# The last output product of a two-block transformer kernel as seven half-size products, with two of its weight sums on GpSimd

## The reference

```python
    merged = (jax.nn.sigmoid(g_diff) * (o_diff @ w_proj_diff[layer])
              + jax.nn.sigmoid(g_mla) * (o_mla @ w_proj_mla[layer]))
    x = x + merged @ w_out[layer]
return rms_norm(x, norm_final)
```

## Time and profile before

| what | value |
|---|---|
| time, median of 3 runs | 1087.87 us (1087.51 to 1088.33) |
| span of the profiled execution | 1085.8 us |
| PE busy | 1072.4 us (99% of the span) |
| DVE busy | 712.5 us (66%) |
| ACT busy | 420.2 us (39%) |
| POOL busy | 0.2 us |
| granted TensorE clock, mean | 0.999 |

### The profile page before, as it was taken

The page is one execution under the profiler, slowest core; times in us unless marked ns, Lnnn a source line. Parts: engine busy times, 40 slices in busy tenths (PEclk is TensorE's granted clock), DMA queues, the critical chain, the costliest instruction groups (busy, mean ns, idle before and its releaser), DMA issues.

```text
span 1085.8 us, 13595 instructions
## 1 busy us (share of the span) xinstructions
PE 1072.4 (99%) x5395; PEld 860.1 (79%) x5397; DVE 712.5 (66%) x1149; ACT 420.2 (39%) x661; POOL 0.2 (0%) x4
## 2 busy tenths in 40 slices
PE   9999999999999999999999999999999999999998
PEld 6777877977878888888888887887776777888886
DVE  6998877868678887854588745654568446464441
ACT  6513655334443223222222234744367443323232
POOL 0000000000000000000000000000000000000000
PEclk9999999999999999999999999999999999999999
DMA  8422122221213323234322234323121222033302
GB/s 279 126 78 79 47 71 79 71 86 39 79 60 106 117 79 105 59 89 129 122 78 88 65 94 143 98 97 117 44 78 40 78 78 78 1 116 117 102 35 78
DMA packets 100239, 95.59 MB, mean 88 GB/s; under 512 B 5952, under 2 KB 91216, under 8 KB 100176
## 3 DMA queue, kind: packets, MB, share of 16 engines
q1 hardware_dynamic: 100000, 94.71, 27.9%
q10 hardware_dynamic: 176, 0.02, 0.0%
HBM read 92.60 MB, written 2.10 MB: 87 GB/s over the span
## 4 chain that ended last, share of the span: by engine, by line
PE 91%; DVE 5%; ACT 2%; issue 1%; DMA 1%; SPq 0%; DVEq 0%; ACTq 0%
PE ring L1036 22%; PE ring L1038 22%; PE ring L1037 22%; PE bank L1036 3%; PE bank L1038 3%; PE bank L1037 3%; PE bank L1500 1%; PE bank L1295 1%; DVE w_lo L1929 1%; PE bank L1267 1%; DMA w_raw<-in_w_in 1%; PE bank L1200 1%; PE bank L1280 1%; PE bank L1524 1%; PE bank L1473 1%
## 5 line engine op out<-in xcount | busy, mean ns | idle before, releaser
L1036 PE MATMUL ring<-act_hi,w_hi 128*128 128x512 f32 (+2 forms) x808 | 320.2, 396 | 0.9 <-DVE xT L2312 0.5
L1038 PE MATMUL ring<-act_hi,w_lo 128*128 128x512 f32 (+2 forms) x808 | 313.5, 388 | 0.0
L1037 PE MATMUL ring<-act_lo,w_hi 128*128 128x512 f32 (+2 forms) x808 | 313.2, 388 | 0.0
L1588 ACT ACTIVATE w_hi<-w_raw 128x2048 fp32r<-128x2048 f32 (+5 forms) x96 | 159.8, 1665 | 249.7 <-PE ring L1038 200.6
L1929 DVE TENSOR_TENSOR w_lo<-w_raw,w_hi 128x2048 fp32r<-128x2048 f32 (+4 forms) x101 | 190.3, 1886 | 4.2 <-ACT w_hi L1588 3.9
L1036 PEld LDWEIGHTS ring<-act_hi,w_hi 128*128 128x128 f32 x808 | 151.8, 188 | 37.1 <-issue 3.9
L1038 PEld LDWEIGHTS ring<-act_hi,w_lo 128*128 128x128 f32 x808 | 151.7, 188 | 31.6
L1037 PEld LDWEIGHTS ring<-act_lo,w_hi 128*128 128x128 f32 x808 | 151.8, 188 | 31.3 <-issue 1.9
L1036 PE MATMUL ring<-hidH,w_hi 128*128 128x512 f32 x176 | 68.5, 389 | 0.0
L1037 PE MATMUL ring<-hidL,w_hi 128*128 128x512 f32 x176 | 68.5, 389 | 0.0
L1038 PE MATMUL ring<-hidH,w_lo 128*128 128x512 f32 x176 | 68.5, 389 | 0.0
(11 more groups left out here) (363 smaller groups left out, 1618.9 us busy)
## 6 DMA issues: line engine op xcount, KB each, us to landing
w_raw<-in_w_in SPq DMA_DIRECT2D x30, 1024.0 KB, 5.3
w_raw<-in_w_up SPq DMA_DIRECT2D x22, 1024.0 KB, 5.1
w_raw<-in_w_out SPq DMA_DIRECT2D x8, 1024.0 KB, 5.1
w_raw<-in_w_down SPq DMA_DIRECT2D x8, 768.0 KB, 4.7
w_raw<-in_w_down SPq DMA_DIRECT2D x8, 640.0 KB, 4.3
w_raw<-in_w_in SPq DMA_DIRECT2D x7, 512.0 KB, 4.7
xin<-in_xt SPq DMA_DIRECT2D x8, 256.0 KB, 4.1
xT<-in_xt SPq DMA_DIRECT2D x2, 1024.0 KB, 6.6
```

What stands on the lines that cost most here:

```text
L1036: pe.matmul(out, ah, bh, start=(first and n == 0), stop=False)
L1037: pe.matmul(out, ah, bl, start=False, stop=False)
L1038: mm = pe.matmul(out, al, bh, start=False, stop=(last and n == len(pairs) - 1))
L1588: return act.activation(out, src, func, **more)
```

## The change

The output product is made with seven products of half size (Strassen's scheme in Winograd's form) in place of eight. `merged` is cut into A11, A12 (channels 0-511 and 512-1023 of tokens 0-255), A21, A22 (of tokens 256-511), and `w_out` into B11, B12, B21, B22. Four sums of weights are formed on the chip: T1 = B12 - B11, T3 = B22 - B12, T2 = T3 + B11, T4 = B21 - T2 (128 x 2048 each), and four sums of activations: S3 = A11 - A21, S1 = A21 + A22, S2 = S1 - A11, S4 = A12 - S2 (128 x 1024 each). The products, in the order of the program, are

0: A11 B11; 1: S3 T3; 2: A12 B21; 3: S2 T2; 4: S1 T1; 5: S4 B22; 6: A22 T4 (with the signs folded into the sums).

Each is made for two groups of 128 tokens, with 12 matmuls a group: 168 in all, where there were 192. The four groups of the residual are still transposed (32 transposes): into the banks of products 2, 5 and 6 and into two ring tiles (`res`). Banks are shared by product n and n + 3, so DVE and ACT must read a bank before the product three later.

T3 and T2 are made on DVE (`t_sum`), **T1 and T4 on GpSimd**, all four S on DVE (`s_sum`). All forms and sums are split into hi and lo like the rest. The scheme's additions of products are on DVE (`s17`, `u_sum`, `v_sum`, `c_sum`, 128 x 512 each, one input from a bank). The scaling by the gain is now a step of its own from SBUF (`scaled`). B12, B22 and B21 are loaded by SP into a raw buffer and into the place of the activations' dead splits.

```diff
+        for c in range(4):
...
+            if c == 3:
+                stage("s_split", 3)
             for kind in ("pd", "pm"):
                 for i in (2 * c, 2 * c + 1):
+                    if (kind, i) == ("pm", 6):
+                        stage("t_sum", "T3")
                     in_tile(kind, i, f"pj{c}")
+                    if (kind, i) == ("pm", 6):
+                        split_form("T3")
+            if c == 1:
+                stage("s_sum", 3)
+
+        both("prod", 0)
         stage("m_flush")
...
+        split_form("B21")
+        stage("t_sum", "T2")
+        both("snap")
+        both("prod", 1)
+        stage("s_sum", 1)
+        stage("s_sum", 2)
+        split_form("T2")
+        stage("s_split", 2)
+        both("s17")
+        for t in range(2):
+            tile(("res", t))
+            stage("res", t)
+        both("prod", 2)
+        stage("c_sum", 2, 0)
+        stage("s_split", 1)
+        stage("c_sum", 2, 1)
+        split_form("T1")
+        stage("s_sum", 4)
+        each("sq_early", 0, 1)
+        both("prod", 3)
+        split_form("B22")
+        stage("s_split", 4)
+        both("u_sum")
+        both("prod", 4)
+        split_form("T4")
+        both("c_sum", 4)
+        both("v_sum")
+        each("sq_early", 2, 3)
+        both("prod", 5)
+        for t in range(2):
+            stage("scaled", t)
+            stage("c_sum", 5, t)
+        each("final", 0, 1)
+        each("scaled", 2, 3)
+        both("prod", 6)
+        for t in range(2):
+            stage("c_sum", 6, t)
+            stage("final", 2 + t)
...
+            wait_split(sp, B11 - 1)
+            quarter_in(raw[(B11 + 1) % 2], 0, 1, raw_in[(B11 + 1) % 2])
+            sp.wait_ge(tile_done, upto(("gm", KD - 1)))
+            quarter_in(b22, 1, 1, block_in[0])
+            quarter_in(b21, 1, 0, block_in[1])
...
+        @block.gpsimd
+        def _(pool):
+            pool.wait_ge(tile_done, upto(("gm", KD - 1)))
+            pool.wait_ge(raw_in[(B11 + 1) % 2], landed[B11 - 1] + 16)
+            pool.wait_ge(raw_in[B11 % 2], landed[B11])
+            pool.tensor_tensor(t1[:], raw[(B11 + 1) % 2][:], raw[B11 % 2][:], ALU.subtract).then_inc(pool_sum, 1)
+            pool.wait_ge(form_sum, 2)
+            pool.wait_ge(w_lo_done, B11 + 1)
+            pool.tensor_tensor(b21[:], b21[:], form_raw["T2"][:], ALU.subtract).then_inc(pool_sum, 1)
...
+                    if name == "T3":
+                        dve.wait_ge(block_in[0], 32)
+                        dve.wait_ge(pool_sum, 1)
+                        TT(form_raw["T3"][:], b22[:], form_raw["T3"][:], ALU.subtract).then_inc(form_sum, 1)
```

More of the change, by code:

```diff
@@ L176, in two_blocks @@
         gated_d, gated_m, merged, m_hi, m_lo = (sem(n) for n in ("gated_d", "gated_m", "merged", "m_hi", "m_lo"))
+        form_sum, pool_sum, s_sum, s_hi, s_lo = (sem(n) for n in ("form_sum", "pool_sum", "s_sum", "s_hi", "s_lo"))
+        prod_mm, snap, part_sum, c_sum = (sem(n) for n in ("prod_mm", "snap", "part_sum", "c_sum"))
         ssf_ready, xo_g, f_var, f_rs, out_act, out_dve, out_done = (
@@ L793, in two_blocks, with split_form, both @@
         attention("mla", 4, "ym", fill)
+        B11 = len(chunks)
+        chunk("B11", k_out2[:, 0:4, 0:512])
+        for name in ("T3", "B21", "T2", "T1", "B22", "T4"):
+            form(name)
+        PROD = ("B11", "T3", "B21", "T2", "T1", "B22", "T4")
+        def split_form(name):
+            stage("w_first", chunk_of[name])
+        def both(kind, *what):
+            for t in range(2):
+                stage(kind, *what, t)
         for c in range(4):
@@ L1542, in _ @@
                     channels(s, f"pj{i // 2}", P * (i % 2), (oH[:, at:at + 4, :], oL[:, at:at + 4, :]), nk=4, part=0 if kind == "pd" else 1)
[L1543 to L1556, removed]
-                        for j in range(4):
[L1558 to L1562, removed]
@@ new lines, in _ @@
+                elif kind == "prod":
+                    n, t = s[1:]
+                    at = slice(P * t, P * t + P)
+                    if n == 0:
+                        pe.wait_ge(m_lo, 4)
+                    elif n in (2, 6):
+                        pe.wait_ge(m_lo, KD)
+                    else:
+                        pe.wait_ge(s_lo, S_SPLITS.index(S_OF[n]) + 1)
+                    if n == 3:
+                        pe.wait_ge(snap, t + 1)
+                    elif n == 4:
+                        pe.wait_ge(part_sum, t + 1)
+                    elif n == 5:
+                        pe.wait_ge(c_sum, t + 1)
+                    elif n == 6:
+                        pe.wait_ge(part_sum, 2 * t + 4)
+                    to = bank[2 * (n % 3) + t]
+                    opened = n in RES_OF
+                    if opened:
+                        half, b0 = RES_OF[n]
+                        for j in range(4):
+                            pe.matmul(to[:, P * j:P * j + P], xT[:, 4 * half + j, b0 + P * t:b0 + P * t + P], ident,
+                                      start=(j == 0), stop=False, is_transpose=True)
+                    lh, ll = left_of(n)
+                    wh, wl = weights(PROD[n])
+                    product(to[:], [((lh[:, k, at], ll[:, k, at]), (wh[:, k, :], wl[:, k, :])) for k in range(4)],
+                            first=not opened).then_inc(prod_mm, 1)
+                elif kind == "res":
+                    b = 2 + s[1]
+                    out = open_bank(s)
+                    for j in range(4):
+                        mm = pe.transpose(out[:, P * j:P * j + P], xT[:, 4 + j, P * b:P * b + P], ident)
+                    mm.then_inc(tile_done, 1)
```

303 lines of the change are left out of this document (201 added, 102 removed).

## The result

The changed kernel takes 1092.26 us (median of 4 runs, 1091.68 to 1092.70), the kernel before in the same sessions 1088.1 us: a ratio of 1.004, 95% interval 1.0026 to 1.0054. It is 4.2 us slower; 3.6 was forecast.

A forecast was written before the change was run, and what follows sets the result against it. TensorE bounds the old stretch, DVE's queue the new end: 1081.35 + 0.8 + 4.2 = 1086.32 against 1082.69, 3.6 us slower. 1087.87 + 3.6 = 1091.5 us; range 1086.0 to 1093.2.

The forecast's parts named there:

- The bare gain of 4.7 us: Output product: 24 fewer matmuls save 5.44 us of TensorE, less 0.73 for the last addition on DVE.
- The queue that I had at 31.7 us: DVE's gapless work from 1040.06 to 1071.8, up to the fourth-last addition, making DVE end last.
- T1's 0.8 us: GpSimd's T1 holds the split of S3, delaying `pd` 6, T3 and the B21 split: 0.8 us.
- T4's 4.2 us: GpSimd's T4 gets in before S2, which starts at 1050.7 in place of 1046.5: 4.2 us in DVE's queue.
- The early gap: Contention with T4 taking DVE's gap before S2 at 1046.5: 3.6 us slower, chance 0.42.
- Rival 2: Contention, but T4 misses the gap before S2 and covers only S1's split: 2.0 us slower, chance 0.20.
- The price of a GpSimd sum: Length of a 128 x 2048 two-input sum on GpSimd: 4.2 us, the middle of 3.8 and 4.57.
- The exclusive end: GpSimd's sums and DVE instructions with two SBUF inputs can't run together; the second waits: 3.6 us slower in total.
- The clock: Rival 5: a 3 us TensorE stall might drop it to 1.2 GHz; nothing added, given 4 us of slack.
- the 4 of my sum: TensorE's slack against DVE by the time of a possible clock fall: 4 us.
- Transfers: B22 and B21 loads, issued together at 1022.4, stay hidden, B22 by 0.6 us before T3 wants it.

The follow-up runs named there:

- the kernel without the sums: Changed kernel with both GpSimd sums left out (products 4 and 6 use B22 and B21 instead): 1086.70 us, 0.9992 of the kernel before.
- T1 alone: Changed kernel with only the second GpSimd sum, T4, left out (product 6 uses B21): 1087.98 us, 1.0000 of the kernel before.
- S3's split late: Changed kernel with S3's split moved behind the reading of `pd` 7, so T1 runs beside bank reads only: 1091.97 us, 1.0039 of the kernel before.
- T4 alone: Changed kernel with only the first GpSimd sum, T1, left out (product 4 uses B22): 1091.27 us, 1.0030 of the kernel before.
- T4 after S2: Changed kernel with GpSimd's T4 also waiting for the sum S2: 1092.51 us, 1.0044 of the kernel before.
- the new order: Changed kernel with scalings ahead of the first final steps and both last additions ahead of the last two: 1090.44 us, 1.0021 of the kernel before.
- the three edits together: Changed kernel with T1 on DVE, GpSimd's T4 beside DVE's bank reads, and the end reordered: 1085.81 us, 0.9979 of the kernel before.

## Why the prediction was right

**TensorE's saving and the DVE queue.** The bare gain of 4.7 us shrinks to 1.34 because DVE ends last: shown by the kernel without the sums, 1.2 us ahead of before with nothing held. The queue that I had at 31.7 us takes 31.5 there, from 1040.65 to the end of the addition at 1071.47 (the third from the end; the prediction calls it the fourth).

**T1's 0.8 us.** Shown by T1 alone, 1.3 us. `pm` 6 waited 1.1 us, not 0.9. As a wait of TensorE it costs nothing (S3's split late); it stands for the delay of DVE's queue. **T4's 4.2 us.** Shown by T4 alone, 4.6 us, and in the row of S2, 4.3 us longer than S1. The early gap was the right one of the two contention cases, but for a wider reason than I gave: GpSimd doesn't need S2's wait to get in (T4 after S2). Rival 2 rested on the opposite.

**The price of a GpSimd sum** was the term mis-sized: 4.63 us in place of 4.2. The upper end, two DVE passes (4.57), was nearly right. The Trainium skill (GPSIMD Engine Reference, section 3.1) has 4497 ns for it; measured 4.63. With 4.63 both sums give 0.9 us more, 4.5 in all, against 4.2 measured in the medians and 4.7 between the two profiled ends (1087.40 and 1082.69). In the profiled execution 0.4 us is older than the change's stretch: the last gate tile is read at 1022.73 in place of 1022.34.

**The exclusive end.** Shown from both sides: a DVE instruction with two SBUF inputs is held, one with an input from a bank isn't, and a GpSimd copy holds too. The Trainium skill (SBUF — State Buffer, "Who interferes with whom") states this, of a DVE instruction with two SBUF inputs against a GpSimd instruction that reads SBUF, and the rows agree with it that the second one is held until the first is done: 1.09 us from GpSimd's end to the end of a 1.22 us instruction.

**The clock.** It did fall, for 12 matmuls: 5.3 us in place of 2.7, and TensorE had the slack that I argued with. An addition that does wait for TensorE starts 0.42 us behind the last matmul (1081.99 and 1082.41 in the new order, 1076.55 and 1076.97 in the three edits together). With T4 alone, at the full clock, DVE adds 4.10 us behind it (1079.38 and 1083.48): a slack of 3.7 us, near the 4 of my sum. In the changed kernel it adds 1.88 us behind it (1082.67 and 1084.55), so some 1.5 us were left. **Transfers** were hidden: T3 starts on DVE as soon as `pd` 7 is read, at 1030.0.

What was not settled: why the clock fell behind the stalls of 3.4 and 4.8 us and not behind that of 3.7, and what the fall costs in the kernel with the new order. In its profiled execution it cost nothing. But of its eleven runs the five with a mean granted clock of 0.998 or more have a median of 1089.9 us and the six at 0.995 or 0.996 one of 1090.7, so a longer fall may count there; no run shows it by itself.

## What to carry to other kernels

Work moved to GpSimd to spare DVE wasn't beside DVE's work but in front of it, wherever DVE read two inputs from SBUF: where DVE's queue has no gap, count it at GpSimd's length, here twice DVE's own (T4, 4.6 us); where DVE would have waited anyway, it costs less (T1, 1.3 us). It held nothing beside DVE instructions with an input from a bank, and the kernel that uses this place was 1.5 us ahead of the one with all sums on DVE. Before saving matmuls, add up the queue of the engine that must combine the parts: of 5.4 us saved, the additions and DVE's queue took all but 1.2 with nothing held. Reordering the end of that queue gave 1.7 to 1.8 us back (the new order, with GpSimd's sums and without them), and moving T4 out of the way of the two-input instructions 3.8.

## What the runs showed of the hardware that was not expected

A DVE instruction held by GpSimd is recorded as busy from where it would have begun (S2: 5.53 us for 1.22), and a held GpSimd instruction too (5.53 and 6.45 for 4.63). GpSimd got in between two DVE instructions that follow each other without a wait (T4 after S2; one case). A GpSimd copy of 128 x 2048 takes 1.90 us, shorter than DVE's two-input pass of 2.28 and 2.4 times shorter than GpSimd's two-input one. A stall of 3.4 us on TensorE was followed by 5.3 us at 1.2 GHz, one of 3.7 us (T4 alone) and those of 1.1 us by none (0.23 us steps behind them), though TensorE was busy before each.
